# Two more pairs of k-tiles as seven block products in a down projection, their activation sums made on GpSimd

## What is computed

```python
def swiglu(x, wg, wu, wd):
    return (jax.nn.silu(x @ wg) * (x @ wu)) @ wd

f = swiglu(rmsnorm(h, ffn1_pre_g[l]), ffn1_wg[l], ffn1_wu[l], ffn1_wd[l])
h = h + FFN_RES_WEIGHT * rmsnorm(f, ffn1_post_g[l])
...
h = h + rmsnorm(mixed, mix_post_g[l])
f = swiglu(rmsnorm(h, ffn2_pre_g[l]), ffn2_wg[l], ffn2_wu[l], ffn2_wd[l])
return h + FFN_RES_WEIGHT * rmsnorm(f, ffn2_post_g[l])
```

## Time and profile before

| | |
|---|---|
| median of 3 runs | 2070.5 us (2070.37 to 2070.84) |
| the profiled execution | 2071.07 us |
| its span | 2069.3 us |
| busy: PE, DVE, ACT, POOL | 2055.6, 1762.5, 1138.7, 27.7 us |
| matmuls | 9262 |
| granted TensorE clock, mean | 0.999 |
| HBM read over the span | 406.14 MB, 197 GB/s |

### The profile page before, as it was taken

One profiled execution on the slowest core, in us unless ns is written; L12 is line 12 of the kernel. 1 busy time (PEld: TensorE's weight loads), 2 busy tenths in 40 slices (PEclk: granted clock), 3 DMA queues, 4 the chain that ended last, 5 costly groups with the idle time before them and its releaser, 6 DMA issues.

```text
span 2069.3 us, 26078 instructions
## 1 busy us (share of the span) xinstructions
PE 2055.6 (99%) x9262; PEld 1699.4 (82%) x9262; DVE 1762.5 (85%) x2137; ACT 1138.7 (55%) x1274; POOL 27.7 (1%) x54
## 2 busy tenths in 40 slices
PE   9999999999999999999999999999999999999998
PEld 8888888888888788888788888888888888888886
DVE  7999999999987758998687555579999999999885
ACT  6565665566555454444566444465656565665553
POOL 0000000000000000100000000000000000000000
PEclk9999999999999999999999999999999999999999
DMA  8666656655657566776555566566666566646564
GB/s 326 220 208 202 202 189 213 207 163 181 206 191 223 162 185 196 205 203 178 178 174 177 184 192 206 194 216 202 200 204 208 197 203 202 204 143 210 196 204 163
DMA packets 211995, 409.51 MB, mean 198 GB/s; under 512 B 15113, under 2 KB 15377, under 8 KB 211520
## 3 DMA queue, kind: packets, MB, share of 16 engines
q1 hardware_dynamic: 209904, 401.26, 60.0%
q0 software_dynamic: 1856, 7.01, 1.4%
q10 hardware_dynamic: 144, 0.04, 0.0%
HBM read 406.14 MB, written 2.11 MB: 197 GB/s over the span
## 4 chain that ended last, share of the span: by engine, by line
PE 97%; DVE 2%; ACT 0%; issue 0%; DMA 0%; SPq 0%; POOL 0%; DVEq 0%; ACTq 0%; POOLq 0%
PE banks L1580 95%; PE banks L1630 2%; DVE wlo L992 1%; DMA raw<-in_ffn_wg_dram 0%; DVE res L1047 0%; DVE h_lo L1272 0%; DVE act_lo L1060 0%; ACT act_hi L558 0%; DVE nat L1175 0%; ACT whi L543 0%; ACT h_hi L739 0%; POOL stat L455 0%; ACT comb L662 0%; DVE comb L1016 0%; SPq L368 0%
## 5 line engine op out<-in xcount | busy, mean ns | idle before, releaser
L543 ACT ACTIVATE whi<-raw 128x1024 fp32r<-128x1024 f32 x579 | 599.3, 1052 | 538.0 <-PE banks L1580 367.3
L992 DVE TENSOR_TENSOR wlo<-raw,whi 128x1024 fp32r<-128x1024 f32 x580 | 691.9, 1216 | 211.7 <-ACT whi L543 209.0
L1580 PE MATMUL banks<-whi,act_hi 128*128 128x512 f32 x1568 | 507.7, 395 | 1.3 <-DVE wlo L992 0.8
L1580 PE MATMUL banks<-whi,act_lo 128*128 128x512 f32 x1568 | 498.3, 389 | 0.0
L1580 PE MATMUL banks<-wlo,act_hi 128*128 128x512 f32 x1568 | 485.2, 389 | 0.0
L1580 PEld LDWEIGHTS banks<-whi,act_lo 128*128 128x128 f32 x1568 | 294.3, 188 | 62.1
L1580 PEld LDWEIGHTS banks<-wlo,act_hi 128*128 128x128 f32 x1568 | 294.2, 188 | 61.6 <-DVE wlo L992 0.3
L1580 PEld LDWEIGHTS banks<-whi,act_hi 128*128 128x128 f32 x1568 | 291.1, 188 | 63.2 <-issue 4.7
L543 ACT ACTIVATE whi<-raw_deep 128x1024 fp32r<-128x1024 f32 x176 | 183.0, 1053 | 171.9 <-DVE raw_deep L1192 161.1
L992 DVE TENSOR_TENSOR wlo<-raw_deep,whi 128x1024 fp32r<-128x1024 f32 x176 | 207.7, 1219 | 7.1 <-ACT whi L543 6.9
L1580 PE MATMUL banks<-whi,h_hi 128*128 128x512 f32 x560 | 179.6, 390 | 0.5 <-ACT whi L543 0.5
(11 more groups left out here) (244 smaller groups left out, 2267.1 us busy)
## 6 DMA issues: line engine op xcount, KB each, us to landing
raw<-in_ffn_wd_dram SPq DMA_DIRECT2D x176, 512.0 KB, 4.7
raw<-in_w_in_dram SPq DMA_DIRECT2D x160, 512.0 KB, 3.7
raw<-in_ffn_wg_dram SPq DMA_DIRECT2D x88, 512.0 KB, 3.7
raw_deep<-in_ffn_wg_dram SPq DMA_DIRECT2D x88, 512.0 KB, 3.7
raw<-in_ffn_wu_dram SPq DMA_DIRECT2D x88, 512.0 KB, 4.5
raw_deep<-in_ffn_wu_dram SPq DMA_DIRECT2D x88, 512.0 KB, 4.6
raw<-in_w_out_dram SPq DMA_DIRECT2D x32, 512.0 KB, 3.6
raw<-in_w_pw_dram SPq DMA_DIRECT2D x16, 512.0 KB, 3.6
```

The costliest lines, as they stand in the source:

```text
L543: nc.scalar.activation(whi[:, j % RING, 0:kts * width], src[:, 0:kts * width], ACT.Copy).then_inc(hi_ready, 1)
L992: nc.vector.tensor_tensor(wlo[:, j % RING, 0:n], raw_slot(j, deep)[0][:, 0:n], whi[:, j % RING, 0:n], ALU.subtract).then_inc(lo_ready, 1)
L1580: return nc.tensor.matmul(o, a, b, **kw)
```

## The change

Pairs 5 and 7 become seven-product pairs in the second half of the columns, in both FFNs. Their four sums of h come from GpSimd (`extra_sums`), which first adds h_hi and h_lo, since h itself is overwritten by h_lo by then; ScalarE makes their high part at the end of the first half, GpSimd the low part. FRONT grows to 17 pairs, REST shrinks to 5. The new tiles lie where `fout` holds column blocks 0 and 1, so the gains and squares of these blocks move behind the last seven-product pair, into REST; the outer copies and the combine of the second half move behind them.

```diff
+EXTRA = (5, 7)
+EXTRA_STEPS = 5
+EXTRA_CHUNKS = max(EXTRA) * SK // KB + 1
+SEVEN_OF = (DOWN_SEVEN, DOWN_SEVEN + EXTRA)
+PLAIN = [q for q in range(DOWN_SLABS) if q not in SEVEN_OF[1]]
+FRONT = PLAIN[:1] + [q for two in zip(PLAIN[1:], SEVEN_OF[1]) for q in two]
...
+        extra_hi, o_ehi = sb("extra_hi", [P, len(EXTRA), 4, P], f32r, over=o_act)
+        extra_lo, o_elo = sb("extra_lo", [P, len(EXTRA), 4, P], f32r, over=o_act + 16 * P * len(EXTRA))
+        extra_full, _ = sb("extra_full", [P, len(EXTRA), SK, SEQ], over=o_ehi)
+        extra_sum, _ = sb("extra_sum", [P, len(EXTRA), 4, P], over=o_elo)
...
+            def extra_sums(f):
+
+                pool.wait_ge(hlo_ready, UP_CHUNKS * f + EXTRA_CHUNKS)
+                for i, q in enumerate(EXTRA):
+                    at0 = EXTRA_STEPS * (len(EXTRA) * f + i)
+                    nc.gpsimd.tensor_tensor(extra_full[:, i], h_hi[:, SK * q:SK * q + SK, :], h_lo[:, SK * q:SK * q + SK, :],
+                                            ALU.add).then_inc(extra_step, 1)
+                    a11, a12, a21, a22 = (extra_full[:, i, k, t * P:(t + 1) * P] for t in range(TT) for k in range(2))
+                    pool.wait_ge(extra_step, at0 + 1)
+                    nc.gpsimd.tensor_tensor(extra_sum[:, i, S5, :], a21, a22, ALU.subtract).then_inc(extra_step, 1)
+                    nc.gpsimd.tensor_tensor(extra_sum[:, i, S7, :], a11, a21, ALU.subtract).then_inc(extra_step, 1)
+                    pool.wait_ge(extra_step, at0 + 2)
+                    nc.gpsimd.tensor_tensor(extra_sum[:, i, S6, :], extra_sum[:, i, S5, :], a11, ALU.subtract).then_inc(extra_step, 1)
+                    pool.wait_ge(extra_step, at0 + 4)
+                    nc.gpsimd.tensor_tensor(extra_sum[:, i, S3, :], extra_sum[:, i, S6, :], a12, ALU.add).then_inc(extra_step, 1)
+                for i in range(len(EXTRA)):
+                    pool.wait_ge(extra_hi_ready, len(EXTRA) * f + i + 1)
+                    nc.gpsimd.tensor_tensor(extra_lo[:, i], extra_sum[:, i], extra_hi[:, i], ALU.subtract).then_inc(extra_lo_ready, 1)
+
             pool.wait_ge(mm_done, UP_SLABS)
             load_gpost(f1_post)
+            extra_sums(0)
             root(2, rpost[0])
...
+                    if q >= DOWN_SLABS - len(EXTRA):
+                        i = q - DOWN_SLABS + len(EXTRA)
+                        act.wait_ge(extra_step, EXTRA_STEPS * (len(EXTRA) * f + i + 1))
+                        nc.scalar.activation(extra_hi[:, i], extra_sum[:, i], ACT.Copy).then_inc(extra_hi_ready, 1)
                 for i, q in enumerate(FRONT):
                     quad(1, HALF_SLABS + 2 * i, q)
-                    if i == 4:
-                        squares_of(0, C11)
-                    if i == 6:
-                        squares_of(1, C12)
                 for k in range(len(REST)):
                     hi_at(REST2 + k)
-                    if k == 1:
+                    if k == 2:
+                        squares_of(0, C11)
+                        squares_of(1, C12)
+                        act.wait_ge(squared, 2 * TT * BLK * f + 2 * TT)
                         outer_copies(1)
...
-                    if i == 3:
-                        gain(0, C11)
-                    if i == 5:
-                        gain(1, C12)
                 for k in range(len(REST)):
                     lo_at(REST2 + k)
                     if k == 1:
+                        dve.wait_ge(wsum_used, down_seven(f, 1, len(SEVEN_OF[1])))
+                        gain(0, C11)
+                        gain(1, C12)
+                    if k == 3:
                         combine(SUMMED + 2, 0)
...
+                        if q in EXTRA:
+                            sums = [t[:, EXTRA.index(q)] for t in (extra_hi, extra_lo)]
+                            pe.wait_ge(extra_lo_ready, len(EXTRA) * f + EXTRA.index(q) + 1)
+                        else:
+                            sums = [t[:, i] for t in (down_hi, down_lo)]
+                            pe.wait_ge(asumlo_ready, ASUMS * f + len(SEVEN) + i + 1)
```

More of the change, by code:

```diff
@@ L89 @@
 DOWN_SEVEN = (9, 11, 13, 15, 17, 19)
-PLAIN = [q for q in range(DOWN_SLABS) if q not in DOWN_SEVEN]
-FRONT = PLAIN[:1] + [q for two in zip(PLAIN[1:], DOWN_SEVEN) for q in two]
+EXTRA = (5, 7)
[4 more added lines that the diff above has]
+FRONT = PLAIN[:1] + [q for two in zip(PLAIN[1:], SEVEN_OF[1]) for q in two]
 REST = [q for q in PLAIN if q not in FRONT]
@@ L95 @@
 CONVERT = {0: (0,), 1: (1,), 2: (2,), 3: (3, 4), 4: (5,), 5: (6,), 6: (7,), 7: (8,), 8: (9,), 10: (10,)}
-SEVENS = len(SEVEN) * SUMMED + 2 * len(DOWN_SEVEN)
+SEVENS = len(SEVEN) * SUMMED + len(SEVEN_OF[0]) + len(SEVEN_OF[1])
 ASUMS = len(SEVEN) + len(DOWN_SEVEN)
@@ L158, in build @@
         o_dsum = o_act + 4 * TT * 2 * CW
+        extra_hi, o_ehi = sb("extra_hi", [P, len(EXTRA), 4, P], f32r, over=o_act)
+        extra_lo, o_elo = sb("extra_lo", [P, len(EXTRA), 4, P], f32r, over=o_act + 16 * P * len(EXTRA))
+        extra_full, _ = sb("extra_full", [P, len(EXTRA), SK, SEQ], over=o_ehi)
+        extra_sum, _ = sb("extra_sum", [P, len(EXTRA), 4, P], over=o_elo)
+        assert o_elo + 16 * P * len(EXTRA) <= o_dsum
         down_hi, _ = sb("down_hi", [P, len(DOWN_SEVEN), 4, P], f32r, over=o_dsum)
@@ L254, in build @@
         gpost_full = sem("gpost_full")
+        extra_step, extra_hi_ready, extra_lo_ready = sem("extra_step"), sem("extra_hi_ready"), sem("extra_lo_ready")
         stored = sem("stored")
@@ L520, in _ @@
             root(7, rstd)
+            extra_sums(1)
             root(8, rpost[0])
@@ L710, in quad @@
                 def quad(half, n, q):
-                    if q in DOWN_SEVEN:
-                        seven = down_seven(f, half, DOWN_SEVEN.index(q))
+                    if q in SEVEN_OF[half]:
+                        seven = down_seven(f, half, SEVEN_OF[half].index(q))
                     hi_at(n)
-                    if q in DOWN_SEVEN:
+                    if q in SEVEN_OF[half]:
                         act.wait_ge(wsum_ready, 4 * seven + 3)
                     hi_at(n + 1)
-                    if q in DOWN_SEVEN:
+                    if q in SEVEN_OF[half]:
                         act.wait_ge(wsum_ready, 4 * seven + 4)
@@ L723, in outer_copies @@
                 def outer_copies(half):
-                    act.wait_ge(wsum_used, down_seven(f, half, len(DOWN_SEVEN)))
+                    act.wait_ge(wsum_used, down_seven(f, half, len(SEVEN_OF[half])))
                     nc.scalar.activation(comb[:, C11, :], banks[:, 4 * half + M1, :], ACT.Copy)
@@ L1762, in quad @@
                 def quad(half, n, q):
-                    if q in DOWN_SEVEN:
-                        i = DOWN_SEVEN.index(q)
+                    if q in SEVEN_OF[half]:
+                        i = SEVEN_OF[half].index(q)
                         acts = [[k_tile(t, 2 * q + k, m) for t in (h_hi, h_lo)] for m, k in ((0, 0), (0, 1), (1, 1))]
-                        pe.wait_ge(asumlo_ready, ASUMS * f + len(SEVEN) + i + 1)
+                        if q in EXTRA:
[4 more added lines that the diff above has]
+                            pe.wait_ge(asumlo_ready, ASUMS * f + len(SEVEN) + i + 1)
                         seven_products(down_seven(f, half, i), down0 + n + 1, n % RING, 1 - half, i == 0,
-                                       i == len(DOWN_SEVEN) - 1, acts, [down_hi[:, i], down_lo[:, i]], down_wsum_lo)
+                                       i == len(SEVEN_OF[half]) - 1, acts, sums, down_wsum_lo)
                     else:
```

## The result

| | before | changed |
|---|---|---|
| median of the runs, us | 2070.6 (2070.1 to 2070.97, 17 runs) | 2074.82 (2074.16 to 2075.64, 17 runs) |
| profiled execution, us | 2071.07 | 2074.67 |
| its span, us | 2069.3 | 2072.9 |

The ratio is 1.0021, with a 95% interval of 1.0013 to 1.0028: 4.2 us slower, 2.2 us above the forecast of 2072.6, inside its range of 2068.4 to 2075.8, and 0.1 us past the 4.1 us that were to part "no change" from "slower". The direction was right and the size was half of what it is. The forecast's own bounds ended at 2074.6; that 2074.8 lies in the range is owed to rival 2's price, which set the upper end.

The account below looks back on a forecast made before the run. TensorE was taken to bound the kernel, busy 2055.6 of 2069.3 us. Matmuls -2.7, GpSimd's sums +3.6, FRONT rounds 0 and tail +1.2 gave +2.1 on 2070.5, so 2072.6 us, range 2068.4 to 2075.8.

Parts of the forecast that it names:

- The forecast's own bounds: Whole kernel: GpSimd waits of 1.2 to 5.0 us and a tail of 0.6 to 1.8 give 2069.6 to 2074.6 us.
- rival 2: At 485 and 1844 us GpSimd holds VectorE for its operations' whole length: 3.1 us per FFN, 2075.2 us; chance 0.22.
- Matmuls: Second half of the columns, pairs 5 and 7, both FFNs: 12 matmuls removed, -2.7 us, all on the path.
- Two more FRONT rounds at 0: FRONT: two more weight sums per FFN keep pace, 9.7 us a round against TensorE's 10.2; cost 0.
- Rival 3: FRONT loses its pace: late DMAs cost up to 0.5 us in each of four more rounds, 2074.6 us; chance 0.06.
- The bound of 0.5 us for a late transfer: FRONT: a round in which the DMA lands late could cost 0.5 us at most, counted in the range.
- The sums of h: Near 485 and 1844 us GpSimd's ten reading operations delay VectorE, TensorE 1.8 us late per FFN: +3.6 us (1.2 to 6.2).
- Twice that if the inputs are read one after the other: 3.2 us: VectorE's loss beside GpSimd's ten operations: twice the 1.6 us floor, which has both inputs read at once at 0.78 ns per column.
- The lead of 1.4 us: VectorE's lead over TensorE at the next pair's first slab, subtracted from its loss: 3.2 - 1.4 = 1.8 us late.
- Rival 1: GpSimd gives way at its sums of h and VectorE pays nothing: 2069.0 us, 2067.8 if the tail hides; chance 0.22.
- The tail: REST, last slab of each down stage: third square before its whi makes wlo 0.6 us late, +1.2 us for both FFNs.
- The sum by that page, +4.7: Whole change, with GpSimd's ten operations priced by the skill page at 2.2 ns a column, 4.5 us: total +4.7 us.

Follow-up runs that it names:

- kernel 3: The changed kernel with ScalarE's third square moved behind the last whi and GpSimd's ten sums moved to the turn of the column halves; 2067.97 us, ratio 0.9987.
- kernel 9: The changed kernel unaltered, profiled once more as a single execution; 2074.9 us beside 2071.05 for the kernel before.
- kernel 6: The changed kernel with GpSimd's ten sums replaced by ten copies of the same widths, one input instead of two; 2069.97 us, ratio 0.9997.
- kernel 2: The changed kernel with GpSimd's ten sums moved to the turn of the column halves, where VectorE is idle; 2069.16 us, ratio 0.9993.
- kernel 1: The changed kernel with ScalarE's squares of column block 2 moved behind the last whi of the down stage; 2073.55 us, ratio 1.0013.
- kernel 4: The kernel before with GpSimd's ten sums added at the changed kernel's place, results unused, nothing else moved; 2076.12 us, ratio 1.0026.

## Why the prediction came out as it did

**Matmuls: right.** 9250, and kernel 3, which has the other costs taken away, is 2.7 us under the kernel before.

**Two more FRONT rounds at 0: right.** VectorE's waits on the DMA in the second FFN's rounds stay between 0.7 and 1.0 us from round to round (1.07 and 0.89 in the earlier trace rows); they do not grow. In the first FFN those behind the late one are 0.35 to 1.70 us, in no rising order, and TensorE has no gap beside them. Rival 3 falls. The bound of 0.5 us for a late transfer is what the profiled execution showed once (0.46), and kernel 9 shows that it isn't the rule.

**The sums of h: mechanism and places right, size too small.** This is the step that failed: "Twice that if the inputs are read one after the other: 3.2 us." I had the price of one input from the earlier trace rows and doubled it. For one input kernel 6 confirms it; two inputs cost 1.00 and 1.09 us for 512 columns, about 2.1 ns a column and 2.7 times the price of one, and 0.14 to 0.27 (0.23 in the mean) for 128. VectorE lost 3.9 us, not 3.2. The lead of 1.4 us then did what the sum said, 3.90 - 1.4 = 2.5 us, which is the 2.49 of the trace, and a restart of 0.12 that I had not counted makes 2.6 per FFN in place of 1.8. Two FFNs: +5.2, not +3.6.

The two waits show that the accounting by place was right too: the adds that start before the first wlo has ended (484.08 to 486.45) take 1.00, 0.14 and 0.26 us from VectorE, and TensorE's first gap grows by 1.4 us, from 0.23 to 1.62. The rest gives 1.10 at the next pair.

**Rival 1** (GpSimd gives way) falls: ten additions on GpSimd, and VectorE's rows beside them are stretched, 3.9 us in all. **Rival 2** (GpSimd holds VectorE for the whole length) had the wrong length and nearly the right price: by the lengths of kernel 2's rows the ten adds last 2 x 1.28 + 8 x 0.46 = 6.2 us, and VectorE loses 3.9 beside them, about 0.2 us less for each. It was put at 3.1 us of wait per FFN, with 2.8 as the point from which it decides; 2.6 were measured, so it does not decide, but it came nearer than the 1.8 of the forecast. The length less about 0.2 us fits all the operations that read: 1.28 and 0.46 us for the adds, 0.60 for the copy of 512 columns, and the select of 0.28, for which wlo lost 0.08. The rows of before allowed this reading as well as one by the column, but none of them had the length of an add. The Trainium skill's rule (SBUF — State Buffer, Who interferes with whom), that the second of the two is blocked for the whole of the first, fits the rows for two inputs nearly (1.0 to 1.1 of 1.28 us) and those for one input less well (0.3 to 0.4 of 0.60); the 0.2 us between them is not in it. The Trainium skill's other page (GPSIMD Engine Reference, Performance versus the Vector engine) gave an estimate of 2.2 ns a column, and kernel 2's adds of 512 and 128 columns, 1.28 and 0.46 us, are 0.82 / 384 = 2.1 ns a column apart. The sum by that page, +4.7, was the nearest to the measured +4.2.

**The tail: right.** 0.6 us per FFN was forecast, 0.63 came (0.52 or 0.53 and the restart), at the wlo behind the third square, and without it kernel 1 is 1.27 us faster than the changed kernel and kernel 3 1.19 us faster than kernel 2.

**The sum** by what was measured: -2.7 + 5.2 + 1.3 = +3.8 us, against +4.2 by the medians. The remaining 0.4 stays open. The small gaps in the first FRONT round are of that kind, but they were 0.46 us in one profile of the changed kernel and 0.13 in the other, and kernel 4, which has no such round, is 0.2 above its sum too.

The chance for "slower by over 4.1" was 0.23, and the time came out 0.1 us past that line. The ends of the price had been 1.6 and 4.5 us of VectorE's time and the point of decision 4.2; a middle taken from a doubled price without a row for a second input deserved less than the 0.50 it had.

## What to carry to other kernels

Work that reads on GpSimd is free only where VectorE is idle or far enough ahead: here the same ten adds cost TensorE 2.6 us at a place with no lead, 0.75 where VectorE was ahead by less than they took, and nothing at the turn of kernels 2 and 3, where it waits. Before moving work to an idle engine, look for the engine that shares something with it, write down that engine's lead over the bound at the place, and subtract; beside VectorE's two-input instructions the price here was the length of the added add less about 0.2 us. A version with fewer matmuls can be had at once from a slower one by asking only where its side work runs: kernel 3 has all of the change's work and is 6.9 us faster than it.

## What the hardware showed that was not expected

- Two inputs of a GpSimd add cost VectorE's two-input instructions about three times what one input costs: 1.0 to 1.09 against 0.30 to 0.41 us for 512 columns, up to 0.27 against 0.1 for 128. GpSimd's own length behaves the same way, 1.28 against 0.60 us for 512 columns (kernel 6's copy at 484.11 us took 0.60).
- A memset on GpSimd (0.52 us for 512 columns, 0.20 for 128) costs VectorE nothing at all.
- Where VectorE's stream has no gaps, the rows look as if GpSimd got its turn once per instruction of VectorE: adds of 0.46 us last 1.33 to 1.43 beside VectorE instructions of 1.22 and 0.46 to 0.60 beside its short sums. So ten short adds spread further beside long instructions, and fewer of them fall before a given point.
- Each of these waits of TensorE costs 0.10 to 0.13 us beyond the wait itself: two matmuls behind it take 0.57 us to the next start in place of 0.45.
